# Gathering the result rows of the last two token tiles by index, in two parts, in a one-core encoder step

## The reference

```python
# x: residual stream; h = rms_norm(x)
g_sel = argmax(h @ w_rg + b_rg)                  # one of 4 groups
top_v, top_i = top_k(e_logits[g_sel], 2)         # 2 of its 8 experts: 32 experts in all
top_w = softmax(top_v) * g_prob
act = silu(h @ w_g[e]) * (h @ w_u[e])            # 1024 -> 128, per expert
out = sum over the 2 experts of (act * top_w) @ w_d[e]   # 128 -> 1024
x = x + out
y = rms_norm(x, norm_final_g)
```

## Time and profile before

| what | us |
|---|---|
| median of 3 runs | 1278.8 (1276.46 to 1279.06) |
| the profiled execution's own time | 1278.63 |
| its span in the trace | 1276.8 |
| outside the span | 1.83 |
| PE busy | 1223.0 (96%) |
| DVE busy | 918.7 (72%) |
| ACT busy | 512.2 (40%) |
| POOL busy | 440.9 (35%) |

### The profile page before, as it was taken

The page is one execution under the profiler, slowest core; times in us unless marked ns, Lnnn a source line. Parts: engine busy times, 40 slices in busy tenths (PEclk is TensorE's granted clock), DMA queues, the critical chain, the costliest instruction groups (busy, mean ns, idle before and its releaser), DMA issues.

```text
span 1276.8 us, 21392 instructions
## 1 busy us (share of the span) xinstructions
PE 1223.0 (96%) x7563; PEld 1066.7 (84%) x7563; DVE 918.7 (72%) x2179; ACT 512.2 (40%) x1117; POOL 440.9 (35%) x740
## 2 busy tenths in 40 slices
PE   6999999999999999998999999999999979998995
PEld 6999999999999999998777667999788858887752
DVE  5657888888999998884667776332666668886747
ACT  6655223232322112324656564100432247765634
POOL 5803575666774115654000000210011233432320
PEclk9999999999999999999999999999999989999998
DMA  7201332222213221102000131944221469999749
GB/s 270 75 30 53 92 72 80 43 79 42 71 43 124 86 84 53 35 1 94 11 1 17 44 98 55 344 133 164 116 83 49 151 228 340 359 341 338 294 165 374
DMA packets 79456, 163.84 MB, mean 128 GB/s; under 512 B 12417, under 2 KB 48081, under 8 KB 78209
## 3 DMA queue, kind: packets, MB, share of 16 engines
q1 hardware_dynamic: 64977, 128.84, 29.8%
q0 software_dynamic: 12656, 27.62, 6.5%
q10 hardware_dynamic: 1728, 6.10, 1.2%
HBM read 137.86 MB, written 39.21 MB: 139 GB/s over the span
## 4 chain that ended last, share of the span: by engine, by line
PE 82%; DMA 7%; DVE 3%; POOL 2%; ACT 2%; SPq 2%; issue 1%; POOLq 0%; ACTq 0%; DVEq 0%
PE bank L921 12%; PE bank L922 12%; PE bank L923 12%; PE bank L1134 5%; DMA region_h<-in_wd 4%; PE bank L1116 3%; PE bank L1218 3%; PE bank L1212 3%; PE bank L1350 3%; PE bank L1052 2%; PE bank L1229 2%; PE bank L1230 2%; PE bank L1231 2%; DMA region_q<-expert_rows_scratch 2%; PE bank L1214 2%; PE bank L1365 1%
## 5 line engine op out<-in xcount | busy, mean ns | idle before, releaser
L1968 DVE MAX8 small<-region_kv 128x8 f32<-128x272 f32 (+4 forms) x241 | 190.2, 828 | 47.6 <-DVE region_kv L1973 47.5
L921 PE MATMUL bank<-h_hi,w_hi 128*128 128x384 f32 (+1 forms) x576 | 196.1, 340 | 0.0
L922 PE MATMUL bank<-h_lo,w_hi 128*128 128x384 f32 (+1 forms) x576 | 196.0, 340 | 0.0
L1973 DVE MATCH_REPLACE8 region_kv<-small,region_kv 128x272 f32<-128x272 f32 (+4 forms) x241 | 195.5, 819 | 0.0
L923 PE MATMUL bank<-h_hi,w_lo 128*128 128x384 f32 (+1 forms) x576 | 194.4, 338 | 0.0
L921 PE MATMUL bank<-w_hi,h_hi 128*128 128x256 f32 x448 | 128.8, 288 | 1.0 <-ACT region_q L1518 1.0
L2331 POOL TENSOR_TENSOR w_lo<-w_stage,w_hi 128x512 fp32r<-128x512 f32 x64 | 80.8, 1293 | 140.6 <-ACT w_hi L1457 140.5
L923 PE MATMUL bank<-w_hi,h_lo 128*128 128x256 f32 x448 | 125.9, 281 | 0.0
L922 PE MATMUL bank<-w_lo,h_hi 128*128 128x256 f32 x448 | 125.9, 281 | 0.0
L923 PEld LDWEIGHTS bank<-h_hi,w_lo 128*128 128x128 f32 x576 | 108.7, 189 | 0.0
L922 PEld LDWEIGHTS bank<-h_lo,w_hi 128*128 128x128 f32 x576 | 108.2, 188 | 0.6
(11 more groups left out here) (350 smaller groups left out, 3061.2 us busy)
## 6 DMA issues: line engine op xcount, KB each, us to landing
w_stage<-in_w_in SPq DMA_DIRECT2D x72, 256.0 KB, 3.2
region_kv<-in_xa SPq DMA_DIRECT2D x16, 512.0 KB, 6.1
region_h<-in_wg SPq DMA_DIRECT2D x15, 512.0 KB
region_h<-in_wu SPq DMA_DIRECT2D x15, 512.0 KB
region_h<-in_wd SPq DMA_DIRECT2D x15, 512.0 KB
region_q<-in_wd SPq DMA_DIRECT2D x12, 512.0 KB
region_q<-in_wg SPq DMA_DIRECT2D x12, 512.0 KB
region_q<-in_wu SPq DMA_DIRECT2D x12, 512.0 KB
```

What stands on the lines that cost most here:

```text
L921: mm(out, st_hi(k), mv_hi(k), start=(k == 0), stop=False)
L922: mm(out, st_hi(k), mv_lo(k), start=False, stop=False)
L1968: nc.vector.max(m8[:, q, :], x).then_inc(dve_c, 1)
L1973: nc.vector.match_replace(x, m8[:, q, :], x, TAKEN).then_inc(dve_c, 1)
```

## The change

The rows of tiles 7 and 8 are no longer loaded by SP. POOL gathers them by index out of `y_d`, in two parts. The early part holds the rows whose expert is 0 to 27: for tile 7 it is issued behind the scatter of expert 29, for tile 8 behind the scatter of expert 30, that is, ahead of the scatter of expert 31. The late part holds the other rows and is issued after all scatters have landed. An index of 4096 and above is skipped, so each part writes only its own rows into `y2[t]`. DVE works out both lists at the start of the expert stage (`row_lists`, six operations on 128x4 numbers). Before all this SP fills the whole of `y_d` with zeros (9.4 MB, in pieces of 1 KB), behind the loads of the first three caches. SP loads seven tiles, 0 to 6. POOL sums tiles 8 and 6 in place of DVE, PE sums 1, 7, 3, 5, DVE 0, 2, 4, and tiles are finished and stored in the order 0, 1, 8, 7, 2, 3, 4, 5, 6.

```diff
+E_LATE = 28
+T_EARLY = 7
...
+        y2_in = [(tile_in[t], tile_seen[t] + 32) for t in range(T_EARLY)] + [(st_in[0], 64 + 64), (st_in[1], 64 + 64)]
+        POOL_SUM = (8, 6)
+        FINAL = [0, 1, 8, 7, 2, 3, 4, 5, 6]
+        PE_SUM = [1, 7, 3, 5]
+        DVE_SUM = [0, 2, 4]
...
             for b in range(3):
                 cache_in(b)
+
+            sp.wait_ge(zero_ready, 3)
+            sp.dma_start(y_d.rearrange("(p n) (q d) -> p (n q) d", p=P, d=256),
+                         zero[:, 0:256].unsqueeze(1).to_broadcast([P, 8 * TOK // P, 256])).then_inc(wo_in, 16)
...
-            for t in range(NT):
+            for t in range(T_EARLY):
                 sp.dma_start(y2[t], y_d[2 * P * t:2 * P * (t + 1), :].rearrange("(p q) d -> p q d", q=2)).then_inc(tile_in[t], 16)
-            for t in range(NT):
-                sp.wait_ge(fin_ready, t + 1)
+            for n, t in enumerate(FINAL):
+                sp.wait_ge(fin_ready, n + 1)
...
+            def row_lists():
+
+                nt = NT - T_EARLY
+                late_e, late_r = view(nflat, 1424 + 4 * nt, nt, 2), view(nflat, 1424 + 6 * nt, nt, 2)
+                row = pairs[:, T_EARLY:NT, :, 0]
+                ts(late_e, r_if[:, T_EARLY:NT, :], float(E_LATE), float(SENT), ALU.is_ge, ALU.mult)
+                link(ts(late_r, r_rank[:, T_EARLY:NT, :], float(P), float(SENT), ALU.is_ge, ALU.mult))
+                link(tt(late_e, late_e, late_r, ALU.max))
+                link(ts(late_r, row, 2.0 * SENT, None, ALU.add))
+                link(stt(out=early_rows, in0=late_e, scalar=float(SENT), in1=row, op0=ALU.add, op1=ALU.add))
+                tt(late_rows, late_r, late_e, ALU.subtract).then_inc(gidx_ready, 1)
+
             expert_lower(0)
+            row_lists()
             overflow_table()
...
             combine(0)
-            for t in range(2, NT, 2):
-                combine(t)
-                if t >= 4:
-                    final(t - 3)
-                final(t - 2)
-            for t in range(NT - 2, NT):
+            final(0)
+            combine(2)
+            final(1)
+            combine(4)
+            for t in FINAL[2:]:
                 final(t)
...
+            def rows_back(t, rows):
+                for q in range(2):
+                    pool.indirect_dma_start(out=y2[t][:, q, :], out_offset=None, in_=y_d,
+                                            in_offset=bass.IndirectOffsetOnAxis(ap=rows[:, t - T_EARLY, q:q + 1], axis=0),
+                                            bounds_check=2 * TOK - 1, oob_is_err=False).then_inc(y2_in[t][0], 16)
...
+                    if y == NE - 3:
+                        pool.wait_ge(gidx_ready, 2)
+                        pool.wait_ge(dn_done, E_LATE)
+                        for s in range(3):
+                            pool.wait_ge(y_out[s], 16 * ((E_LATE - s + 2) // 3))
+                    if NE - 3 <= y < NE - 1:
+                        rows_back(T_EARLY + y - (NE - 3), early_rows)
...
             nc.gpsimd.memset(pjunk[:, 2:3], 0.0).then_inc(over_end, 1)
+            for s in range(3):
+                pool.wait_ge(y_out[s], 16 * ((NE - s + 2) // 3))
+            for t in (8, 7):
+                rows_back(t, late_rows)
+            for t in POOL_SUM:
+                pool.wait_ge(*y2_in[t])
+                link(tt(x2[:, t, :], y2[t][:, 0, :], x2[:, t, :], ALU.add))
+                tt(x2[:, t, :], y2[t][:, 1, :], x2[:, t, :], ALU.add).then_inc(over_end, 1)
```

28 lines of the change are left out of this document (17 added, 11 removed).

## The result

The changed kernel takes 1280.8 us (median of 9 runs, 1277.8 to 1281.7), the kernel before 1277.6 us in 9 runs (1276.4 to 1280.4). The ratio is 1.0021 with an interval of 1.0013 to 1.0029, so 2.7 us more. The interval leaves out 1, so this small loss is real. The forecast was 1279.3 us, no change beyond about 0.2%; the measurement lies at that limit, 1.5 us above the forecast and inside its range. As a change it is further off: the forecast added 0.7 us to the 1278.63 us of the profiled execution, and 2.7 us came. The prediction knew three runs of the kernel before, with a median of 1278.8 us; the median of nine is 1.2 us lower. The profiled execution took 1281.5 us, span 1279.8; that of before had a span of 1276.8, so the two profiles differ by 3.0 us.

What follows compares the result with a forecast made beforehand. At the end DMA engines and DVE are both nearly full, within a few us. Later scatter, earlier loads and collisions laid out give span 1276.8 + 0.7 = 1277.5, so 1278.63 + 0.7 = 1279.3 us; range 1275.4 to 1282.0.

Steps and rivals of the forecast that it cites:

- the layout: Last stage laid out engine by engine, with POOL and DVE excluding each other: last final ends at 1273.8, store at 1277.5.
- Something ahead of the expert stage: Before the expert stage, the `y_d` fill (22 us, at slowest 123) and `row_lists` on DVE are hidden: price 0.
- The last scatter, issue: On POOL, two tile 8 gathers ahead make expert 31's scatter start at 1235.3, 1.7 us later.
- The last scatter, queue: On the DMA queue, 0.9 MB ahead of expert 31's scatter is mostly moved by 1236.3; 0.3 us is left.
- rival B: Tile 8's early rows on POOL's queue hold the last scatter: delay 5.8 us, span 1281.3, about 1282.3 us; chance 0.17.
- The loads: SP's seven loads: first used at 1245.6, then 2.48 us each; tile 6 in at 1262.4, 2.4 us earlier.
- The late rows: POOL's late gathers after the last scatter end at 1245.1, just ahead of tile 0; POOL's sum of tile 8 begins at 1245.6.
- rival C: Tile 8's late gathers are served behind SP's 7 MB, POOL's sums start at 1262.4: 1281.7 us; chance 0.05.
- The collisions: In the last stage, POOL sums and DVE operations reading two SBUF tensors exclude each other: 3.6 us more.
- The stretched sum 0 and final 4: Signs on DVE in the last stage: these operations should last above 1.3 us, up to 3.6, beside POOL's sums.
- The end: DVE ends last, its last finals without a gap: final 6 to 1273.8, the store ends at 1277.5.
- D: Behind SP's start, bytes must move anyway, so no effect: 29.3 us at 421 GB/s, to about 1271; given no chance.

Runs made afterwards that it cites:

- 5: The kernel before with only the 9.4 MB zero fill of `y_d` and the waits on it added: ratio 1.0005 to the kernel before.
- 2: The changed kernel with the sums of tiles 8 and 6 back on DVE, none on POOL: ratio 1.0034 to the kernel before.
- 6: The changed kernel with tile 7 finished later, behind tile 4, and PE's sums in order 1, 3, 7, 5: ratio 1.0020 to the kernel before.
- experiment 1: The changed kernel with only tile 8 gathered, its early part behind expert 29's scatter; tile 7 is SP's third load: ratio 1.0001 to the kernel before.
- 11: The changed kernel with early gathers one expert sooner (experts 0 to 25) and tile 7 finished behind tile 4: ratio 0.9995 to the kernel before.
- experiment 7: The kernel before with only DVE's last-stage order altered, final 0 directly behind sum 0; no gathers by index, no fill: ratio 1.0002.
- 3: The changed kernel with early gathers one expert sooner, behind the scatters of experts 28 and 29, for experts 0 to 25: ratio 1.0009 to the kernel before.

## Why the prediction came out as it did

The forecast of no change beyond 0.2%, 1279.3 us, is good to 1.5 us, but partly by luck: errors cancelled. Against the forecast span of 1277.5 SP started 3.0 us too late, and from there to the end it took 0.7 us less than forecast (36.9 in place of 37.65); the sum is the 2.3 us by which the span is longer. The 3.0 are 3.8 us of landing and 0.1 of issue, less the 0.8 us by which the stage's input came sooner. Behind SP's start a wait of 2.8 us that the layout did not have stands against fewer collisions and a shorter end.

**Something ahead of the expert stage: right.** The fill costs nothing that can be told (5). The rate of small stores in the earlier trace rows was too dark a bound: 29.6 us to landing, not 123. DVE's six small operations of `row_lists` show nothing, as the earlier trace rows had it; they were not tried by themselves.

**The last scatter, issue: right.** Forecast 1.7 us later relative to expert 31's rows. Measured: the scatter starts 3.31 us behind the start of DVE's last half (1231.23 to 1234.54), before 1.53 (1232.05 to 1233.58), so 1.78.

**The last scatter, queue: the step that failed.** "On the queue 28 / 32 of 1 MB stands ahead of it, 0.9 MB or 2.2 us at 421 GB/s, mostly moved by 1236.3 [...] I take 0.3 us for what is left." Measured 4.08 us (8.35 less 4.27) in the change's profile; 1.75 and 2.14 in the two other profiles with the same queue (2 and 6, from 6.02 and 6.41). The reckoning took the mean rate of sixteen full engines up to the landing. The rows show a tail instead: the engines fall idle one after the other, and the last works alone. It also left out that the scatter of expert 30 and `gfin` were in flight beside the rows; for `gfin` only rival B says so. The three landings are single executions, and experiment 1 landed at 6.1 us with nothing right ahead of its scatter, so how much of the 1.75 to 4.1 us is the queue's alone stays open.

**Rival B by its mark.** It was to decide "from a landing at about 1241.9 on", and SP started at 1242.89; the delay of 5.86 us is B's bound. So in the profile B's place and price came about, and only the 0.82 us upstream and the time behind SP kept the end from B's 1283.1. By the runs, 1280.8 lies about midway between the forecast and B's centre of 1282.3. One outcome does not test a chance of 0.17, but the mark that was named for B, a landing behind 1241.9, was passed.

**The loads: right.** Tile 6 was forecast 22.55 us behind SP's start (1239.85 to 1262.4); POOL starts its sum at 1265.06, 22.2 us behind it. The pace of the earlier trace rows held.

**The late rows: wrong.** POOL's sum of tile 8 was laid out 5.75 us behind SP's start, and came 11.90 behind it (1254.79). The step assumed that gathers of an eighth of the rows land soon. They land 9 to 13 us behind their issue, behind or beside SP's 7 MB, longer than the 6.36 us of a full gather in the earlier trace rows. The mark of rival C, POOL's sum of tile 8 behind 1250, was passed as well. This is half of rival C: the rows are not served last, but far from first. Tile 7's late rows, for which the layout had no wait, and PE's slow sum of them held DVE for 2.81 us.

**The collisions: right in kind, too many.** The exclusion read from the earlier trace rows is there: DVE's sum 4 takes 2.34 us and final 2 2.41, and POOL's first sum 3.05 beside them, where 1.23, 1.29 and 2.35 are the free durations. The Trainium skill's rule of the exclusive port pair ("SBUF — State Buffer", SBUF: two separate sides) fits these rows. On DVE it is 1.11 + 1.12 = 2.2 us. The layout had the end 3.6 us later by collisions; here only the 1.12 of final 2 reach the end, since the 1.11 of sum 4 lie ahead of DVE's wait of 2.81. POOL began its sums 6 us later than laid out and met fewer of DVE's. The stretched sum 0 and final 4 that the prediction named as signs did not come (1.23 and 1.28 us).

**The end: right for the changed kernel.** DVE works without a gap from final 7 on and ends last; the store follows. The layout had 3.7 us from the end of the last final to the end (1273.8 to 1277.5), and it is 3.1 (1276.73 to 1279.8). Of D the prediction said "the bytes are not the bound": experiments 6 and 11, drained 33.8 and 34.2 us behind SP's start, bear this out for the changed kernel. For the kernel before, experiment 7 shows that bytes and DVE stand together at about 38 us. The prediction's "two resources lie within a few us of each other" was the right reading there, and it was not carried to what an order alone would give.

## What to carry to other kernels

A transfer placed ahead of the one that everything waits for delays it until the last DMA engine has finished, which here took longer than its bytes over the mean rate. Putting it one step earlier was the better place here (3, 11), rather than right before or right behind. Late parts of a gather that are small still took 9 to 13 us beside a queue of megabytes, so finish their tile last. A delay taken away upstream is worth only what the rest of the stage lets through: 5 us of way brought 0 to 1.5 us. When GpSimd does work near the end, add its closing drain (here 7.8 us) to the candidates for what ends last.
